# Plain fp32 products on raw weights, in place of three fp32r products on split operands, in a three-block transformer kernel

## The reference

```python
# mix1: h = rms_norm(x); proj = h @ w_in  (1024 x 3072)
#       4 differential heads and 8 plain heads of attention on 256 tokens; x += y @ w_out
# moe:  grouped top-2 routing over 32 experts, silu(x@gate)*(x@up) @ down
# lru:  h = rms_norm(x)*(1+scale)+shift; xb, gb = split(h @ in_w)  (1024 x 2816)
#       conv of width 4, two gates r and i, a = exp(log_a), scan h = a*h + u
#       y = h * gelu(gb); x += gate * (y @ out_w)             (1408 x 1024)
# peer0: product-key retrieval of 128 rows of (u, v) for each token
# fox:  q, k, v, f, og = split(h @ in_w)  (1024 x 4112); decay = cumsum(log_sigmoid(f))
#       16 heads of attention with the decay as bias; x += gate * ((o * sigmoid(og)) @ out_w)
# peer1: as peer0
```

## Time and profile before

| what | us |
|---|---|
| median of 3 runs | 2306.54 |
| lowest and highest | 2304.33, 2306.97 |
| span of the profiled execution, first to last instruction | 2305.2 |
| mix1, from its first to its last matmul | 9.1 to 210.5 |
| lru, both blocks, first to last matmul | 507.5 to 671.1 |
| fox, first to last matmul | 1386.4 to 1592.5 |
| PE busy | 1867.9 (81%) |
| DVE busy | 1309.6 (57%) |

### The profile page before, as it was taken

The page is one execution under the profiler, slowest core; times in us unless marked ns, Lnnn a source line. Parts: engine busy times, 40 slices in busy tenths (PEclk is TensorE's granted clock), DMA queues, the critical chain, the costliest instruction groups (busy, mean ns, idle before and its releaser), DMA issues. The chain is left out here.

```text
span 2305.2 us, 20305 instructions
## 1 busy us (share of the span) xinstructions
PE 1867.9 (81%) x6462; PEld 996.1 (43%) x6462; DVE 1309.6 (57%) x3175; ACT 615.8 (27%) x1400; POOL 744.7 (32%) x707
## 2 busy tenths in 40 slices
PE   6987889959877888777868788988788887787777
PEld 4555323329555444333323337656444433332333
DVE  4454300037267567667676656545756667677664
ACT  3343111124622222222221214543222222222222
POOL 1000154410103433443544420330444344444542
PEclk9998899979988999998989897998899889898989
DMA  8843999958548999999999977543999999999997
GB/s 303 317 166 139 385 399 399 402 197 230 225 154 333 409 409 411 421 421 422 421 422 415 421 300 249 183 168 100 354 409 409 411 421 422 421 420 419 418 418 293
DMA packets 211846, 786.03 MB, mean 341 GB/s; under 512 B 29243, under 2 KB 89403, under 8 KB 145948
## 3 DMA queue, kind: packets, MB, share of 16 engines
q0 software_dynamic: 85408, 547.20, 57.8%
q1 hardware_dynamic: 126332, 237.53, 28.6%
HBM read 806.56 MB, written 13.98 MB: 356 GB/s over the span
## 5 line engine op out<-in xcount | busy, mean ns | idle before, releaser
L1873 PE MATMUL psum<-peer_rows,peer_diag 128*128 128x512 f32 x2048 | 972.8, 634 | 254.9 <-ACT peer_diag L1929 254.9
L1971 POOL DMA_INDIRECT peer_rows<-in_peer_uv,peer_expert x512 | 583.8, 1140 | 874.7 <-PE psum L1873 676.4
L2074 DVE CUSTOM_DVE_ANT_0 peer_rows<-peer_rows,peer_norm_h 128x1024 f32<-128x1024 f32 x512 | 619.9, 1225 | 424.7 <-DMA peer_rows<-in_peer_uv,peer_expert 424.5
L1873 PEld LDWEIGHTS psum<-peer_rows,peer_diag 128*128 128x128 f32 x2048 | 409.3, 203 | 802.0 <-issue 498.2
L1929 ACT ACTIVATE peer_diag<-ident,peer_weight 128x128 f32<-128x128 f32 x512 | 164.9, 390 | 741.8 <-DVE peer_weight L2084 712.5
L1218 PE MATMUL psum<-moe_ring,moe_W 128*64 128x512 f32 x640 | 143.7, 594 | 16.7 <-DMA moe_ring<-in_moe_w,moe_piece_i 13.0
L1852 PE MATMUL psum<-peer_norm_hT,peer_q_raw 128*128 128x256 f32 x512 | 126.6, 406 | 20.6 <-DMA peer_q_raw<-in_peer_q 17.4
L1852 PEld LDWEIGHTS psum<-peer_norm_hT,peer_q_raw 128*128 128x128 f32 x512 | 103.7, 205 | 47.7 <-DMA peer_q_raw<-in_peer_q 24.0
L1294 POOL COPY moe_W<-moe_X 128x512 f32 x40 | 24.5, 623 | 258.2 <-issue 196.4
L1922 ACT ACTIVATE peer_dots<-peer_dots 128x4 f32<-128x4 f32 (+1 forms) x140 | 28.6, 204 | 249.3 <-DVE peer_dots L2074 249.0
L1218 PEld LDWEIGHTS psum<-moe_ring,moe_W 128*64 128x64 f32 x640 | 46.2, 137 | 110.6 <-issue 110.5
(11 more groups left out here) (444 smaller groups left out, 2213.8 us busy)
## 6 DMA issues: line engine op xcount, KB each, us to landing
moe_ring<-in_moe_w SPq DMA_DIRECT2D x192, 512.0 KB, 11.6
mix_mod_w<-in_mod_w SPq DMA_DIRECT2D x32, 768.0 KB, 7.3
peer_q_raw<-in_peer_q SPq DMA_DIRECT2D x32, 512.0 KB, 24.8
fox_w_raw<-in_fox_in SPq DMA_DIRECT2D x32, 512.0 KB, 5.1
mix_w_raw<-in_w_in SPq DMA_DIRECT2D x24, 512.0 KB, 8.6
lru_mod_w<-in_mod_w SPq DMA_DIRECT2D x16, 768.0 KB, 7.5
fox_mod_w<-in_mod_w SPq DMA_DIRECT2D x16, 768.0 KB, 6.6
lru_in_raw<-in_lru_in SPq DMA_DIRECT2D x22, 512.0 KB, 7.2
```

The lines of the kernel that those rows point to most:

```text
L1873: ins = pe.matmul(Y(t, c), diag[:, j % 2, k, :], R[:, place_of(m), D + c * BANK:D + (c + 1) * BANK], start=m % PICKS == 0, stop=m % PICKS ...
L1971: pool.indirect_dma_start(R[:, place_of(m), :], None, uv, bass.IndirectOffsetOnAxis(ap=expert[:, t, at:at + 1], axis=0))\
L2074: dve.tensor_tensor_reduce(here, here, norm.h[:, t, :], 1.0, 0.0, ALU.mult, ALU.add, dots[:, t, at:at + 1]).then_inc(dotted, 1)
```

## The change

The three split stages multiply plain float32: one matmul takes the place of three. Rounding and subtracting go, for weights and activations alike. `Norm` has one form, and its transposes use the banks in another numbering. The mixer's weights stand in one ring of 16 places of 512 KB (8 landing places, and 4 + 4 places for the halves, before), lru's input weights in 12 places, and its output weights in 11, one for each piece. A place comes free when PE has used it. In lru's second block SP issues all output weights behind the modulation pieces; four of them stood ahead before.

```diff
-        self.stream = Stream(core, ctx, name + "_w", P, self.BL * BANK, land=8)
+        self.stream = Stream(core, ctx, name + "_w", P, self.BL * BANK, land=16)
...
-    def load(self, sp, base, j, copy):
-
-        wait_past(sp, self.split, base + j - self.land + 1)
+    def load(self, sp, j, copy):
+
+        wait_past(sp, self.used, j - self.land + 1)
         copy(self.raw[:, j % self.land, :]).then_inc(self.landed[j % self.land], 16)
...
-def three(pe, out, ah, al, bh, bl, start, stop):
-
-    pe.matmul(out, ah, bh, start=start, stop=False)
-    pe.matmul(out, ah, bl, start=False, stop=False)
-    return pe.matmul(out, al, bh, start=False, stop=stop)
...
     def piece(self, pe, n):
...
-        wh, wl = self.stream.ready(pe, 0, n)
+        w = self.stream.ready(pe, n)
...
-                ins = three(pe, self.core.psum[:, banks[t], 0:width], ah[:, k, tok], al[:, k, tok], wh[:, cols], wl[:, cols],
-                            k == 0, k == KD - 1)
+                ins = pe.matmul(self.core.psum[:, banks[t], 0:width], a[:, k, tok], w[:, cols], start=k == 0, stop=k == KD - 1)
...
-    def y_low(self, dve, half):
-        for n in range(2 * half, 2 * half + 2):
-            dve.wait_ge(self.yT_act, n + 1)
-            dve.tensor_tensor(self.y_to(self.yTl, n), self.y_tile(n), self.y_to(self.yTh, n).bitcast(F32), ALU.subtract)\
-               .then_inc(self.yT_dve, 1)
+    def y_by_dve(self, dve, half):
+        dve.wait_ge(self.y_turned, 2 * half + 2)
+        dve.tensor_copy(self.y_to(2 * half + 1), self.y_tile(2 * half + 1)).then_inc(self.yT_dve, 1)
...
-        out = Stream(core, ctx, "lru_out", P, D, land=4)
-        yh, yl = (core.sbuf(ctx, n, [P, LBLK, SEQ], F32R) for n in ("lru_yh", "lru_yl"))
+        out = Stream(core, ctx, "lru_out", P, D, LBLK)
...
-                for b in range(out.land):
-                    lru_out(b)
                 for q in range(mods.slots):
                     mods.load(sp, q)
                 mods.load_bias(sp)
                 for q in range(mods.slots, mods.total):
                     mods.load(sp, q)
-                for b in range(out.land, LBLK):
+                for b in range(LBLK):
                     lru_out(b)
```

More of the change, by code:

```diff
@@ L186, in act, with dve @@
         act.activation(self.stat[:, 2, :], self.stat[:, 1, :], ACT.Sqrt).then_inc(self.std_ready, 1)
[L187 to L190, removed]
         for n in range(1, 2 * NT, 2):
[L192 to L203, removed]
+            self.affine(act, n, self.hT[self.at(n % 2, n // 2)]).then_inc(self.hT_act, 1)
+    def dve(self, dve):
         chain = Chain(dve, self.chain_sem)
@@ L305, in subtract @@
[L305 to L315, removed]
@@ L353, in pe @@
                 cols = slice(k * self.m, (k + 1) * self.m)
-                ins = three(pe, self.bank(b), wh[:, cols], wl[:, cols], self.core.hTh[:, k, :], self.core.hTl[:, k, :],
-                            k == 0, k == KD - 1)
+                ins = pe.matmul(self.bank(b), w[:, cols], self.norm.hT[:, k, :], start=k == 0, stop=k == KD - 1)
             ins.then_inc(self.stream.used, 1)
@@ L724, in stage_mix1 @@
         width = 3 * D
-        core.halves(ctx, "mix1")
         norm = Norm(core, ctx, "norm1", d["norm1_g"][0])
@@ L849, in _ @@
             def _(act):
-                norm.act(act, weights=lambda: m.round_to(act, 1))
-                m.round_to(act, 4)
+                norm.act(act)
                 mods.act(act)
@@ L894, in _ @@
             def _(dve):
[L895 to L896 removed]
+                norm.dve(dve)
                 dve.wait_ge(curve_done, 1)
@@ L1496, in stage_lru @@
         with ExitStack() as inner:
-            core.halves(inner, "lru")
             xb = core.sbuf(inner, "lru_x", [P, LBLK, CONV - 1 + SEQ])
@@ L1544, in _ @@
                 def _(dve):
-                    norm.dve(dve, weights=lambda: win.stream.subtract(dve, 0, 0))
+                    norm.dve(dve)
                     chain = Chain(dve, conv_chain)
@@ L1602, in stage_lru @@
         flat = lambda v: v.rearrange("p b t -> p (b t)")
-        def pieces_after(c):
-            return range(max(0, end(c - 2)) + out.land, min(end(c - 1) + out.land, LBLK))
         with nc.Block() as block:
@@ L1674, in _ @@
                         act.activation(chunk(xc, c), chunk(rr, c), ACT.Square).then_inc(squared, 1)
-                def high(c):
-                    act.wait_ge(y_ready, c + 1)
-                    act.copy(chunk(yh, c), chunk(xc, c)).then_inc(yh_ready, 1)
-                def rounds(c):
-                    for b in pieces_after(c):
-                        out.round(act, 0, b)
                 for c in range(CHUNKS):
@@ L1708, in _ @@
                 dve.tensor_scalar(nsp[:, 1, :], nsp[:, 0, :], -1.0, None, ALU.mult).then_inc(nsp_ready, 1)
-                for b in range(out.land):
-                    out.subtract(dve, 0, b)
                 def square(c):
@@ L2125, in stage_fox @@
         width = 4 * D + MAPS
-        core.halves(ctx, "fox")
         norm = Norm(core, ctx, "fox_norm", d["fox_g"], mod=2)
```

231 lines of the change are left out of this document (53 added, 178 removed).

## The result

The changed kernel took 2332.4 us (median of 4 runs, 2326.2 to 2335.6), the kernel before 2306.8 in the runs beside it. The ratio is 1.0109, with a 95% interval from 1.0088 to 1.0131: slower by some 25 us, where 124 us less were forecast. The profiled execution has a span of 2333.7 against 2305.2, with a mean granted clock of 0.923 against 0.912, so the clock does not explain it.

A forecast was written before the change was run, and what follows sets the result against it. PE was taken to set the pace mostly, with DMA binding parts of mix1 and lru's first block. Gains of 31 (mix1), 32 (lru) and 61 (fox) sum to 124 us, from span 2305.2 to 2181, median 2182; range 2163 to 2205.

The forecast's parts named there:

- the price of a product: Split stages: plain product 0.436 us for 512 columns, 0.216 for 256, against 0.706 and 0.354; wrong if over 0.5.
- The fourth rival: Every product: a plain one needs four passes of the fp32r price, 0.942 us against 0.706; about 2382 us, chance 0.03.
- The stalls of the second turns: Step 7 of both attentions: without four subtractions on DVE, 6.6 us falls to 1 to 2; gain 5 in mix1, 4.8 in fox.
- Step 0 of mix1: mix1's start, bound by DMA: step 0 at 84 to 87 us, gain 5, bounds 0 and 13.
- lru's first block: lru: PE meets DMA and the block ends when the gate weights land, about 561 instead of 583; gain 21, bounds 17 and 28.
- The start of fox: PE starts products when the norm's transposes end, at 1392.1 instead of 1394.90; gain 2.8 us.
- The decay's chain: fox before step 0: chain of 17.3 us falls to 12.5, about 5 being rounding, subtraction and waits for them.
- Waits for modulation pieces in mix1: PE's waits for these transfers in mix1 should grow from 11 us to over 20.
- moe and the peers: Stages already plain float32: change costed at nothing; forecast wrong if they move by more than 3 us.
- Step 0 of fox: fox: step 0 starts some 43 us behind the norm's transposes instead of 74.4, 31 us earlier.
- The first rival: Freed time returns as waits for loads, clock drops and latency chains; gain 90, 2216 us, chance 0.13.
- The third: Rival: mix1's first part not bound by DMA, lru's gate weights moving beside the others; 2162 us, chance 0.14.

The follow-up runs named there:

- run 1: Kernel before with only the product changed: one plain float32 matmul on the rounded halves for three fp32r, all split work kept; 2357.5 us, ratio 1.0217.
- runs 2 and 3: Changed kernel, projection products of mix1, lru, fox read one scratch tile: one plain matmul each (2334.5 us), then three fp32r matmuls each (2275.5 us).
- run 6: Changed kernel with back-to-back runs of plain and fp32r matmuls ahead of the first stage; at 512 columns 0.846 us plain, 0.233 fp32r.
- run 3: Changed kernel with every projection product of mix1, lru and fox as three fp32r matmuls on one scratch tile, no split work; 2275.5 us, ratio 0.9864.
- run 4: Changed kernel with every projection product of mix1, lru and fox as two fp32r matmuls on one scratch tile; 2194.4 us, ratio 0.9508.
- run 7: Kernel before with the splits of the first four output weights moved from step 6 of both attentions to steps 8 to 11; 2290.8 us, ratio 0.9927.
- runs 7 and 8: Kernel before with output-weight splits spread over steps 8 to 11 (2290.8 us); then also forget gate's projection turned around and high halves multiplied first (2281.7 us).
- run 5: Changed kernel with the ring back to 8 places and four output weights of lru loaded ahead of the modulation pieces; 2331.7 us, ratio 1.0108.

## Why the prediction was wrong

**The failed step is the price of a product**: "The plain one costs about two of the fp32r matmuls, not three." It took each record of the earlier trace rows for a matmul of the program. The pace of a record, 0.436 and 0.216, was read rightly; a product has two of them, 0.872 and 0.432, 3.7 passes of fp32r. So the group of fox is busy for 149.7 us where 73 were forecast. The rows on record said so. The earlier trace rows has x6 for a modulation piece that issues three matmuls. The last line of the earlier trace rows has x4 for scores, of which a step issues two matmuls. And in the groups of the kernel before, the gates of lru show 124 records:

```profile
L1634 PE MATMUL psum<-lru_xc,lru_gate_w 128*128 128x256 f32 x124 | 27.0, 380 | 1.1 <-PEq L1507 1.1
```

The program's order has 62 there. Against the 528 split records of fox stand 528 matmuls in the program. One division, 27.0 / 62 = 0.435, would have given the price.

With that price the products lose 332 x 0.166 + 176 x 0.078 = 69 us where the forecast had them gain. Measured: 50 (run 1) and 59 (runs 2 and 3). In run 1 PE waited 7.3 us less for modulation pieces in mix1, and the small products of fox gained 3.7; the rest of the difference stays open.

**The two pages.** The prediction had its rows agree with the Trainium skill's footnote of "Perfetto Trace Analysis", section "Engine Utilization" (half the rate for fp32 in its low/high form), and speak against its page "FP8 and Floating Point Precision", section "TensorE Precision Notes" (four passes). It is the other way round. A record is at about half the rate (0.436 us against 0.2355 for fp32r) and there are two of them, so the product is at nearly four passes: 0.846 / 0.233 = 3.6 in run 6.

**The fourth rival was the right mechanism**, at 0.03, and its size was off: 2382 against 2332. Its price was 0.942 where 0.872 holds, which is 332 x 0.070 = 23 us, and 7 more on the narrow products. It let only 23 us of stalls and starts go, where run 3 puts the removal of the split work at 35. The rest, some 8 us, is loss that didn't come out whole. The condition that it named, a product above 0.706, was met.

**The other steps, by run 4 and the rows after.** The stalls of the second turns: forecast 1 to 2 us left, measured 0.86 and 0.72. Their term of 4.8 to 5 us each was too small: 8.2 and 6.5 in run 7. Step 0 of mix1: forecast at 84 to 87, measured 94.7, and its gain of 5 us didn't come in run 4 either. lru's first block: forecast gain 21; in run 4 the gates start 20.7 us earlier within the stage, and at the plain price 7.9 later. The start of fox: first product as forecast, 3.56 behind the transposes against 3.7. The decay's chain: 12.3 for the forecast 12.5. Waits for modulation pieces in mix1: forecast over 20, measured 12.4, as PE is slower and not faster; at the price of two fp32r matmuls (run 4) they are 26.0. moe and the peers: costed at nothing, and no difference that can be told from their scatter. The sign of being wrong that was set for them, 3 us, was crossed (4.4 and 3.6), but it was smaller than that scatter and told nothing; the sign for the price, 0.5 us a product, was crossed by 0.86 and told all. Step 0 of fox stands 71.1 us behind the transposes for the forecast 43 and the 74.4 before: the 64 wide products ahead of it cost 0.436 more each than forecast, which is 28.

**The first rival** (time given back as waits) is refuted as the cause: PE waits less than before in front of its products, and 12.4 against 12.0 us for the modulation pieces of mix1. **The third** had the price of the forecast and falls with it.

**What stays open.** Run 3 and run 1 put the gain of the removed split work at different sizes: 35 us at the price of three fp32r matmuls, and 25 at the plain price (2357.5 to 2332.4). That a slower PE hides more of the others' work would fit, but no run shows it. How much of the 9 us between runs 7 and 8 belongs to the turned projection was not measured.

## What to carry to other kernels

Before a duration of the trace becomes a price, divide the busy time of a group by the number of instructions that the program issues, not by the records. With 128 weight columns, an fp32 matmul of 256 or 512 moving columns costs more than three fp32r ones, one of 128 or 16 costs less, and the split's own work is worth removing only where it holds PE up. Taking all split work away was worth some 32 to 35 us at the old price. Moving four subtractions from ahead of the maxima, in two places, gave 15 with the split kept. The two don't simply add: in mix1 the move gave more (8.7) than the removal (5.5), where PE waited 16.5 us for modulation pieces against 11.8.

## What the runs showed of the hardware

- A plain float32 matmul leaves two matmul and two weight-load records; an fp32r matmul or a transpose leaves one (16 transposes of the norm, x16 in the row of 1411.94).
- PE can be busy all the time and still fall to half clock: with 16 moving columns the granted clock was 0.50 from 107 to 126 us of run 6. With 16 weight columns and 256 moving it was back at 1.00 from 133 us on.
- fp32r matmuls of 256 and 128 columns have nearly one price, 0.123 and 0.112 us, where 512 columns cost 0.233.
- Shortening a stall of 6.6 us on PE by 5.7 to 5.9 gave about 8.2 us in mix1 and 6.5 in fox. In mix1 the stall had been followed by 6 us at 0.54 of the clock and 6 at 0.89.
- The same products at the start of fox (16 transposes, then 16 products of 16 columns) ran at a granted clock of 0.50 in the changed kernel and 0.84 in run 5, and step 0 came 3.5 us earlier for it.
